# Gate and up projections as seven-product block multiplications, with weight sums and gate scaling on GpSimd

## The reference

```python
xn = rms_norm(h, ffn_norm_g[l])                       # h: 528 x 1024
g = causal_dwconv(xn @ w_gate[l], conv_w[l], conv_b[l])   # width 3 along the tokens, 2816 features
h = h + (gelu(g) * (xn @ w_up[l])) @ w_down[l]        # w_gate, w_up: 1024 x 2816, w_down: 2816 x 1024
```

## Time and profile before

| | us |
|---|---|
| median of 3 runs (1100.14 to 1100.99) | 1100.65 |
| the profiled execution | 1100.07 |
| its span, first to last instruction | 1098.3 |
| PE busy in the span | 1064.2 |
| DVE, ACT, POOL busy | 522.4, 471.3, 123.3 |

### The profile page before, as it was taken

One profiled execution on the slowest core, in us unless ns is written; L12 is line 12 of the kernel. 1 busy time (PEld: TensorE's weight loads), 2 busy tenths in 40 slices (PEclk: granted clock), 3 DMA queues, 4 the chain that ended last, 5 costly groups with the idle time before them and its releaser, 6 DMA issues.

```text
span 1098.3 us, 18457 instructions
## 1 busy us (share of the span) xinstructions
PE 1064.2 (97%) x7668; PEld 1001.0 (91%) x7668; DVE 522.4 (48%) x690; ACT 471.3 (43%) x662; POOL 123.3 (11%) x121
## 2 busy tenths in 40 slices
PE   6998899999999999999999989999999999999997
PEld 6897799999999999999999978999988999888886
DVE  5667645545445545232336576455455544532221
ACT  5775435444444444122237664364344543421110
POOL 1262000111000111000003510000001100000000
PEclk9989999999999999999999899999999999999999
DMA  6311222322322322323321112223223232233212
GB/s 201 103 49 40 77 77 77 103 89 77 114 76 76 105 86 70 103 78 105 104 78 49 39 40 97 96 77 108 84 76 114 77 111 80 76 106 106 72 61 77
DMA packets 93518, 94.30 MB, mean 86 GB/s; under 512 B 3392, under 2 KB 91800, under 8 KB 93480
## 3 DMA queue, kind: packets, MB, share of 16 engines
q1 hardware_dynamic: 92768, 93.01, 26.4%
q0 software_dynamic: 400, 0.58, 0.2%
q10 hardware_dynamic: 312, 0.18, 0.1%
HBM read 91.65 MB, written 2.10 MB: 85 GB/s over the span
## 4 chain that ended last, share of the span: by engine, by line
PE 82%; ACT 8%; DVE 7%; issue 1%; DMA 1%; SPq 0%; POOL 0%; DVEq 0%; ACTq 0%; POOLq 0%
PE slot L443 80%; ACT probs L919 3%; ACT w_hi L337 1%; DVE nmax L1170 1%; DMA x_in<-in_x 1%; ACT rot_s L844 1%; DVE ms_work L1121 1%; DVE probs L1189 1%; DVE w_lo L348 1%; DVE mix_lo L1205 0%; ACT x_hi L778 0%; DVE den L1181 0%; DVE sumsq L1046 0%; DVE sink_arg L1175 0%; ACT pool_hi L852 0%
## 5 line engine op out<-in xcount | busy, mean ns | idle before, releaser
L443 PE MATMUL slot<-x_hi,w_hi 128*128 128x264 f32 (+1 forms) x1552 | 364.1, 302 | 5.4 <-DVE x_lo L1033 2.7
L443 PE MATMUL slot<-x_lo,w_hi 128*128 128x264 f32 (+1 forms) x1552 | 361.0, 300 | 0.0
L443 PE MATMUL slot<-x_hi,w_lo 128*128 128x264 f32 (+1 forms) x1552 | 360.2, 299 | 0.0
L348 DVE TENSOR_TENSOR w_lo<-raw,w_hi 128x2048 fp32r<-128x2048 f32 (+2 forms) x87 | 194.6, 2237 | 247.6 <-ACT w_hi L337 247.6
L337 ACT ACTIVATE w_hi<-raw 128x2048 fp32r<-128x2048 f32 (+3 forms) x89 | 160.8, 1806 | 260.8 <-PE slot L443 259.5
L443 PEld LDWEIGHTS slot<-x_hi,w_hi 128*128 128x128 f32 x1552 | 254.4, 190 | 17.4 <-DVE u_sb L1152 3.9
L443 PEld LDWEIGHTS slot<-x_lo,w_hi 128*128 128x128 f32 x1552 | 253.0, 190 | 7.3
L443 PEld LDWEIGHTS slot<-x_hi,w_lo 128*128 128x128 f32 x1552 | 252.6, 191 | 7.4
L443 PE MATMUL slot<-m_hi,w_lo 128*128 128x264 f32 (+1 forms) x528 | 140.7, 321 | 0.0
L443 PE MATMUL slot<-m_hi,w_hi 128*128 128x264 f32 (+1 forms) x528 | 140.4, 320 | 0.0
L443 PE MATMUL slot<-m_lo,w_hi 128*128 128x264 f32 (+1 forms) x528 | 140.3, 320 | 0.0
(11 more groups left out here) (142 smaller groups left out, 931.3 us busy)
## 6 DMA issues: line engine op xcount, KB each, us to landing
raw<-in_w_gate SPq DMA_DIRECT2D x44, 512.0 KB, 4.6
raw<-in_w_up SPq DMA_DIRECT2D x44, 512.0 KB, 4.4
raw<-in_w_down SPq DMA_DIRECT2D x32, 512.0 KB, 4.3
raw<-in_w_in SPq DMA_DIRECT2D x19, 512.0 KB, 4.9
raw<-in_w_out SPq DMA_DIRECT2D x16, 512.0 KB, 4.5
raw<-in_w_down SPq DMA_DIRECT2D x16, 384.0 KB, 3.6
x_in<-in_x SPq DMA_DIRECT2D x4, 512.0 KB, 7.7
out<-y_out SPq DMA_DIRECT2D x8, 256.0 KB, 3.0
```

The costliest lines, as they stand in the source:

```text
L348: ins = nc.vector.tensor_tensor(w_lo[s][:, a:b], raw[s][:, a:b], w_hi[s][:, a:b].bitcast(f32), ALU.subtract)
L443: ins = nc.tensor.matmul(out_part, w[ws][:, r, cols], a[:, k, tokens], start=first and n == 0 and w is w_hi and a is a_hi, stop=end and w ...
```

## The change

The gate and the up product of each unit are no longer computed block by block. A unit's 1024 x 256 weights and the 528 tokens (516 in the last layer, from token 12) are each seen as 2 x 2 blocks (512 features by 128 columns, 512 features by half the tokens), and the 2 x 2 block product is formed from seven products instead of eight, by Winograd's scheme with shared sums:

- PE runs P1 to P7 (`product`), 12 matmuls each (4 k-blocks x 3 passes), in four PSUM banks; P6, P3 and P7 go on adding in a bank that holds P1, P5 and P6, after ACT has copied that value out.
- The weight operands are two blocks of raw weights, four sums and another raw block. POOL makes the sums in `w_sum` (`operand_sums`, four instructions of 512 elements a unit), one buffer for all units. ACT and DVE split them in four parts (`operand_hi`, `operand_lo`: 1024, 1024, 1024 and 512 elements).
- ACT copies P1, P5, P6 and P4 out of PSUM (`save`), DVE makes the four output blocks with one add each (`add_block`).
- The token operands (t_ext, and t_base in the place of `x_hi`, `x_lo`) are made once a layer, while the out projection ends (`t_sums`, `t_hi`, `t_low`); out tiles come in the order 0, 4, 1, 5, 2, 6, 3, 7.
- The gate tile is scaled by the inverse norm by POOL (`scale_gate`), in place, before the taps; the up tile is not scaled. Each down tile is multiplied by the inverse norm instead (`add_down`: two DVE instructions with `conv` as a buffer).
- `m_hi` and `m_lo` hold 8 tiles instead of 22. The MLP runs in three chunks of 4, 4 and 3 steps, each followed by its four down units; every loop is written out. The convolution's bias moves from L984 into the gelu.
- The weights of the next unit are prepared one unit ahead on ACT and DVE, the sums two units ahead on POOL.

The core of the diff:

```diff
-DOWN_K = [(0, 8), (8, 16), (16, FT)]
-UNITS = U_DOWN + len(DOWN_K) * (D_MODEL // UC)
+CHUNKS = [(0, 4), (4, 8), (8, FI)]
+PLAN = [("plain", u) for u in range(U_FFN)]
+for c, (a, b) in enumerate(CHUNKS):
+    PLAN += [(kind, i) for i in range(a, b) for kind in ("gate", "up")] + [("down", 4 * c + j) for j in range(4)]
+UNITS = len(PLAN)
+UNIT_OF = {item: u for u, item in enumerate(PLAN)}
+MC = 2 * max(b - a for a, b in CHUNKS)
...
+PRODUCTS = {"P1": ("ext", 0, "ext", 0, 1), "P2": ("ext", 1, "ext", 1, 1), "P3": ("base", 2, "ext", 2, 3),
+            "P4": ("ext", 2, "base", 3, 4), "P5": ("base", 0, "base", 0, 2), "P6": ("base", 1, "base", 1, 2),
+            "P7": ("base", 3, "base", 2, 3)}
+ORDER = ("P1", "P5", "P2", "P6", "P3", "P4", "P7")
...
+        def operand(s, n, hi_lo):
+            rows = raw[s][:].rearrange("p k (c m) -> p k c m", c=2)
+            ext = w_ext[s][hi_lo][:].rearrange("p o k m -> p (o k) m")
+            base = w_base[s][hi_lo].rearrange("p o k m -> p (o k) m")
+            sums = w_sum[:].rearrange("p o k m -> p (o k) m")
+            return ((ext[:, 0:8], rows[:, :, 0]), (base[:, 0:8], sums[:, 0:8]),
+                    (base[:, 8:16], sums[:, 8:16]), (ext[:, 8:12], rows[:, 4:8, 1]))[n - 1]
+        def operand_hi(act, l, unit, n):
...
+                    act.wait_ge(*last_user_done(l, unit))
+                else:
+                    act.wait_ge(prod_done, product_count(f - 2, {2: "P6", 3: "P7"}[n]))
+                act.wait_ge(sum_ready, 4 * f + {2: 2, 3: 4}[n])
+            dst, src = operand(s, n, 0)
+            nc.scalar.activation(dst, src, ACT.Copy).then_inc(opnd_hi, 1)
+        def operand_lo(dve, l, unit, n):
+            f, s = ffn_turn(l, unit), unit % 2
+            dve.wait_ge(opnd_hi, 4 * f + n)
+            (dst, src), (hi, _) = operand(s, n, 1), operand(s, n, 0)
+            nc.vector.tensor_tensor(dst, src, hi.bitcast(f32), ALU.subtract).then_inc(opnd_lo, 1)
...
+                def product(name, unit, kks, first, last):
+                    f, s = ffn_turn(l, unit), unit % 2
+                    wk, wn, tk, tn, ready = PRODUCTS[name]
+                    pe.wait_ge(opnd_lo, 4 * f + ready)
+                    if first and name in ("P6", "P3", "P7"):
...
+                    bank = {"P1": (0, 0), "P6": (0, 0), "P7": (0, 0), "P2": (0, 1), "P5": (1, 0), "P3": (1, 0),
+                            "P4": (1, 1)}[name]
+                    dst = slot[(2 if s == 0 else 0) + bank[0]][:, bank[1], 0:width]
+                    w_op = [(w_ext if wk == "ext" else w_base)[s][n] for n in range(2)]
+                    t_op = [(t_ext if tk == "ext" else t_base)[n] for n in range(2)]
+                    for kk in kks:
+                        for n, (w, t) in enumerate(((0, 0), (0, 1), (1, 0))):
+                            ins = nc.tensor.matmul(dst, w_op[w][:, wn, kk], t_op[t][:, tn, kk, 0:width],
+                                                   start=first and kk == kks[0] and n == 0 and name in ("P1", "P2", "P4", "P5"),
+                                                   stop=last and kk == kks[-1] and n == 2, skip_group_check=True)
+                    if last:
+                        ins.then_inc(prod_done, 1)
...
+                for c, (i0, i1) in enumerate(CHUNKS):
+                    for i in range(i0, i1):
+                        for kind in ("gate", "up"):
+                            unit = UNIT_OF[kind, i]
+                            f, sa = ffn_turn(l, unit), 2 if kind == "gate" else 0
+                            if i == i0:
+                                for n in range(2):
+                                    pe.wait_ge(evac[sa + n], ps.before(f"down{c}_{(sa + n + 2) % 4}", l))
+                            else:
+                                pe.wait_ge(block_added, 4 * (f - 1))
+                            if unit > U_FFN:
+                                for name in ORDER:
+                                    product(name, unit, range(4), True, True)
+                                continue
...
+                def operand_sums(unit):
+                    f, s = ffn_turn(l, unit), unit % 2
+                    rows = raw[s][:].rearrange("p (h k) (c m) -> p h c k m", h=2, c=2)
+                    a11, a12, a21, a22 = rows[:, 0, 0], rows[:, 1, 0], rows[:, 0, 1], rows[:, 1, 1]
+                    if f % FT == 0:
+                        pool.wait_ge(filled[ps.slot("out0")], ps.before("out0", l) + 1)
+                    pool.wait_ge(raw_loaded[s], load_turn(l, unit) * 32 + 32)
+                    if f > 0:
+                        pool.wait_ge(opnd_lo, 4 * (f - 1) + 2)
+                    nc.gpsimd.tensor_tensor(w_sum[:, 0], a21, a22, ALU.add).then_inc(sum_ready, 1)
+                    pool.wait_ge(sum_ready, 4 * f + 1)
+                    nc.gpsimd.tensor_tensor(w_sum[:, 1], w_sum[:, 0], a11, ALU.subtract).then_inc(sum_ready, 1)
+                    pool.wait_ge(sum_ready, 4 * f + 2)
+                    if f > 0:
+                        pool.wait_ge(opnd_lo, 4 * (f - 1) + 3)
+                    nc.gpsimd.tensor_tensor(w_sum[:, 2], a12, w_sum[:, 1], ALU.subtract).then_inc(sum_ready, 1)
+                    nc.gpsimd.tensor_tensor(w_sum[:, 3], a21, a11, ALU.subtract).then_inc(sum_ready, 1)
+                def gated(i):
+                    f = ffn_turn(l, UNIT_OF["up", i])
                     for c in range(2):
...
                         pool.wait_ge(gelu_ready, l * FT + i * 2 + (c + 1))
...
+                        pool.wait_ge(block_added, 4 * f + 2 * (c + 1))
                         nc.gpsimd.tensor_tensor(up[c][:, t0:], up[c][:, t0:], conv[c][:, t0:], ALU.mult)\
                           .then_inc(m_ready, 1)
+                width, (na, nb) = half_tokens(l)
...
+                def scale_gate(i, c):
+                    f = ffn_turn(l, UNIT_OF["gate", i])
+                    if i == 0 and c == 0:
+                        pool.wait_ge(evac[ps.slot("ffn_norm")], ps.before("ffn_norm", l) + 1)
+                    pool.wait_ge(block_added, 4 * f + 2 * (c + 1))
+                    rows = gate[c][:, 2 + na.start:2 + nb.stop]
+                    nc.gpsimd.tensor_tensor(rows, rows, rinv[:, na.start:nb.stop], ALU.mult).then_inc(gate_ready, 1)
+                for unit in range(U_FFN - 2, UNITS):
+                    kind, i = PLAN[unit]
+                    if PLAN[unit - 1][0] == "up":
+                        gated(PLAN[unit - 1][1])
+                    if kind == "up":
+                        scale_gate(i, 1)
+                    if unit + 2 < UNITS and not is_plain(unit + 2):
+                        operand_sums(unit + 2)
...
+                def save(f, n):
+                    s = f % 2
+                    if f >= 2:
+                        act.wait_ge(block_added, 4 * (f - 1))
+                    if f % FT == 0:
+                        act.wait_ge(*norm_added(l, 1, KT - 1))
+                    if f % FT == 1:
+                        act.wait_ge(evac[ps.slot("ffn_norm")], ps.before("ffn_norm", l) + 1)
+                    name = save_order(f)[n]
+                    act.wait_ge(prod_done, product_count(f, name))
+                    pair, half, n = {"P1": (0, 0, 0), "P5": (1, 0, 1), "P6": (0, 0, 2), "P4": (1, 1, 3)}[name]
+                    bank = slot[(2 if s == 0 else 0) + pair][:, half, 0:width]
+                    nc.scalar.activation(saved[s][n][:, 0:width], bank, ACT.Copy).then_inc(prod_saved, 1)
+                def tap2(i, c):
+                    act.wait_ge(gate_ready, l * FT + i * 2 + (c + 1))
+                    if i > 0:
+                        act.wait_ge(m_ready, l * FT + (i - 1) * 2 + (c + 1))
+                    tap = R_CW + 2 * FT + 2 * i + c
+                    nc.scalar.activation(conv[c][:, t0:], gate[c][:, 2 + t0:], ACT.Copy, scale=par[:, tap:tap + 1])\
+                      .then_inc(tap2_ready, 1)
...
+                for ch, (i0, i1) in enumerate(CHUNKS):
+                    for i in range(i0, i1):
+                        for kind in ("gate", "up"):
+                            unit = UNIT_OF[kind, i]
+                            f, nxt = ffn_turn(l, unit), unit + 1
+                            ffn = not is_plain(nxt)
+                            if ffn:
+                                operand_hi(act, l, nxt, 1)
+                            save(f, 0)
+                            if kind == "up":
+                                tap2(i, 0)
+                            if ffn:
+                                operand_hi(act, l, nxt, 2)
+                            save(f, 1)
+                            if kind == "up":
+                                tap2(i, 1)
+                            if ffn:
+                                operand_hi(act, l, nxt, 3)
+                                operand_hi(act, l, nxt, 4)
+                            else:
+                                split_hi(act, l, nxt)
+                            save(f, 2)
+                            save(f, 3)
```

(22 more changed lines are left out.)

539 lines of the change are left out of this document (349 added, 190 removed).

## The result

The changed kernel takes 1115.92 us (median of 4 runs, 1114.27 to 1119.53) against 1100.39 of the kernel before (4 runs on the same chip): a ratio of 1.0143, 95% interval 1.0128 to 1.0157. The forecast of 1108 had the sign and the mechanism; the loss is 15.5 us where 7.5 was forecast, and most of the difference is one term, the start of the MLP. The profiled executions have spans of 1112.5 and 1098.3 us, a difference of 14.2.

A forecast was written before the change was run, and what follows sets the result against it. PE bounds the kernel before; DVE and POOL's shared port would bound crowded steps after. From 1100.07: - 62.6 (PE) + 65.0 (waits) + 0.9 (end) + 4 (clock) = 1107.4, median 0.6 above: 1108 us, range 1096 to 1118.

The forecast's parts named there:

- PE's saving: Gate and up products: 84 matmuls a unit, saving 62.6 us over both layers if PE never waits.
- the line: Layer 1 products: 258-column matmuls priced at 0.1194 us by width; if narrower saves nothing, 0.1220, costing 4.8 us.
- The exclusion and its lengths: MLP: DVE reading two SBUF operands and POOL reading SBUF exclude each other; POOL holds its free duration less 0.24 us.
- rival 3: Crowded steps: each holder keeps the port its whole duration, or handovers cost as much; 1137 us, chance 0.10.
- rival 1: Crowded steps: the port is held shorter, ten steps save 20 us; 1088 us, chance 0.20.
- The walk: Middle of a chunk: operations followed in order give a step of 25.95 us, the load landing just before the sums.
- PE's wait: Crowded step: PE waits 3.7 us at P3 in the up unit and 1.7 at P6 in the next gate unit.
- the 14.0 lost: First chunk of layer 0: PE's loss, including what the chunk pays at its start, 14.0 us.
- start term: Start of the MLP: DVE's t operands and low parts end some 0.5 us beyond the 36 matmuls covering them.
- The clock: Crowded steps: PE's gaps lower its granted clock, costing +4 us in all.
- Rival 4: Crowded steps: each 3.7 us gap costs its full 3 us of clock, ten times and more; 1125 us, chance 0.12.
- The end: Down tiles: two DVE instructions instead of one, covered except behind the last tile, +0.9 us.

The follow-up runs named there:

- e6: The changed kernel with POOL writing zeros instead of the weight sums for the first two units of each layer: 1108.5 us, ratio 1.0090.
- e5: The changed kernel with all weight sums replaced by POOL memsets of 512 elements, which read nothing: 1047.8 us, ratio 0.9513.
- e1: The changed kernel with all weight sums replaced by POOL memsets of 1024 elements, which read nothing: 1047.2 us, ratio 0.9501.
- e3: The changed kernel with the gate scaling moved from POOL to DVE, the weight sums staying on POOL: 1113.7 us, ratio 1.0095.
- e8: The changed kernel with the MLP in four chunks of 3, 3, 3 and 2 steps, sums on POOL: 1105.9 us, ratio 1.0041.

## Why the prediction was right and wrong, point by point

**PE's saving.** Right in kind. By the chain of after, 84 matmuls of 264 columns and 84 of 258:

```profile
320.09 10.21 PE slot L761 x84
...
863.83 10.13 PE slot L761 x84
```

A matmul of 258 takes 0.1206 us, between the line (0.1194) and the other end (0.1220): 22 x 84 x 0.0012 = 2.2 us too much saved, inside the range given. One of 264 takes 0.1215 here, not 0.1220, which gives 0.8 us back.

**The exclusion and its lengths.** Right. A crowded stretch of after, DVE and POOL:

```profile
224.43 1.79 DVE L1608 SCALAR_TENSOR_TENSOR work<-gate,par_all,work 128x528 f32<-128x528 f32 x1
226.26 1.68 DVE L1610 SCALAR_TENSOR_TENSOR work<-gate,par_all,work 128x528 f32<-128x528 f32 x1
227.86 1.78 DVE L433 TENSOR_TENSOR w_ext_lo<-raw,w_ext_hi 128x512 fp32r<-128x512 f32 x1
```

```profile
225.74 1.64 POOL L903 TENSOR_TENSOR w_sum<-raw,w_sum 128x512 f32<-128x512 f32 x1
227.34 1.76 POOL L904 TENSOR_TENSOR w_sum<-raw 128x512 f32<-128x512 f32 x1
```

They alternate, a tap or a low part and a sum every 1.6 to 1.8 us. Whole durations of a tap and a sum would add up to 0.76 + 1.3 = 2.06; by the forecast, 0.76 and a hold of 1.02, it is 1.78. So rival 3 falls, and so does rival 1, whose step was 24. So does what the Trainium skill, page "SBUF — State Buffer", section "SBUF: two separate sides", says of the whole instruction: the lock is seen, the length differs. Steps i lie 26.1 to 26.2 us apart in layer 0 (201.64 to 227.86, by DVE's last low part of an up unit) and 25.8 to 26.0 in layer 1; forecast 25.95, and some 0.1 less in layer 1. The walk did not have the load in the chain (above); the step came out right with nothing put on it.

**PE's wait.** Right in place, wrong in number and size. PE's timeline at P3 of an up unit and the clock behind it:

```profile
220.56 0.56 PE L761 MATMUL slot<-t_ext_hi,w_hi 128*128 128x264 f32 x1 [4.43 <-ACT sumsq L1187]
```

```profile
216.00:220.00 4.00, 0.13 (x2) 0.00 (x0) 2.22 (x2) 1.54 (x2) 3.50 (x3) 1.00 0.08 25
220.00:224.00 4.00, 3.44 (x16) 3.47 (x17) 3.96 (x5) 2.78 (x6) 1.77 (x2) 0.57 0.00 0
```

There is one wait of 3.2 to 4.8 us a step instead of 3.7 and 1.7. The clock fell to 0.57 behind it, and the slower PE used up the second wait: that is how I read it, no run separates the two. The sum is the step's excess over PE either way, as the text had it. The second and third chunks took 93.8 and 68.5 us in layer 0, where 94.4 and 68.0 were forecast with the clock, and 159.9 together in layer 1, where it was 160.4.

**The first chunk: the mis-sized term.** The forecast with all its terms is 98.5 us in layer 0: PE's 82.0, the 14.0 lost, 0.9 for the clock, and 1.6 by which the kernel before exceeds PE's price in its own product stage, which the forecast left in the time that it started from. Measured: 101.3. In layer 1 it is 80.2 + 14.7 (its two crowded steps lose 0.35 more each) + 0.9 + 1.1 = 96.9, and 100.7 was measured, 0.8 of it the width. So 2.8 and 3.0 us are missing, just what e6 takes away. The step of the prediction that failed is its start term, t operands "some 0.5 beyond the 36 matmuls that cover them, 4.4 us": the walk added DVE's free durations there and forgot that POOL's sums for the second unit run at the same time, with the very exclusion that the forecast is built on. PE waited 3.15 and 2.71 us instead of 0.5, and lost clock behind it. The mechanism was right; it was left out in one place.

**The clock.** +4 was put on the crowded steps, none on the start. Rival 4, a clock under 0.9 in the MLP, falls: the product stages have 0.93 to 0.96. The 2.3 us in the row with the attention part and the 2.0 gained before the first gate matmul are no more than other executions scatter by. 1.8 of the former lie in two attention stretches that take 83.6 us together in one layer and 85.5 in the other of after, 84.5 and 83.6 in the kernel before, and 83.0 to 85.6 over all thirteen traces, with and without the change. The first gate matmul comes between 171.7 and 175.3 us in them. That the two nearly cancel here is luck.

**The end** was forecast at +0.9 and measured at +1.0.

## What to carry to other kernels

Before work is given to an idle POOL, add its time to DVE's: where DVE's instructions read two SBUF operands and POOL's read SBUF, their times added up here, and DVE is the faster one (0.69 us against 1.3 for the same sum). Walk the stages at the edge of the changed loop with the same care as the loop itself, with every engine's work in them; there arose what the forecast missed. Where work is too dense for one engine, look at how it lies against stages in which that engine is idle: cutting the MLP in four chunks instead of three gave 10 us in three versions. It has an end: five chunks lost 9 us against four.

## What the runs showed of the hardware that I had not expected

POOL's memset writes to SBUF beside DVE's two-operand instructions with neither held: all of them take 0.52 to 0.53 us for 512 elements (e5) and 0.95 to 0.96 for 1024 (e1), with DVE's w_ext_lo at its free 0.682. The Trainium skill, page "SBUF — State Buffer", section "SBUF: two separate sides", has two-input operations excluded only by a GpSimd operation that reads SBUF; e1 agrees.

An instruction of DVE that reads a single tensor can be held too: L1539 reads one SBUF tensor of 264 columns and a factor for each partition, and takes 1.27 us beside POOL's sum (in after, e3 and e8), 0.36 without it (e6). Adds that take one operand from PSUM stay at 0.42 in the crowded steps.
